# First block's recurrence, index scores and attention in pieces between the parts of its input product, with GpSimd making every second low half from the eighth group on

## The chip, the cores and the metric

The kernel runs on one core of one Trainium2 chip. The metric is the device time of one execution in microseconds; lower is better. The profile is one execution taken by the hardware profiler.

## What is computed

Two transformer blocks, one after the other, on 256 tokens of width 2048, all in float32. The change touches only the first block:

```python
mod = silu(c) @ ada_w + ada_b;  shift, scale, gate = split(mod)
h = rms_norm(x, norm_g) * (1 + scale) + shift
proj = h @ w_in            # 256 x 2048 times 2048 x 9296
a_q, a_k, a_v, a_g, i_q, i_k, i_w, r_q, r_f, r_i, r_g = split(proj)
q, k = rope(rms_norm(a_q)), rope(rms_norm(a_k))       # 8 heads of 128
qi, ki = rope(i_q), rope(rms_norm(i_k))               # 16 index heads of 64
score = sum_h relu(qi_h . ki) * wi_h                  # the 64 best keys of a query are kept
o_a = softmax(q k^T over the kept keys) v * silu(a_g)
o_r = rms_norm(gated recurrence(silu(r_q), lb + (1-lb) sigmoid(r_f), r_i)) * silu(r_g)
x = x + gate * (concat(o_a, o_r) @ w_out)
```

The recurrence is computed in chunks of 64 tokens, with a lower bound lb from a softmax over two rows.

## The kernel before

**Large products.** A product of a 256-row operand with a weight matrix is cut into groups of 512 columns, and a group into 8 parts of 256 rows of the weight (two tiles of 128). SyncE fetches the weight in chunks of 1 MB, two parts each, into a ring `raw` of 4 chunks. To keep float32 accuracy each weight is split: ScalarE writes the rounded high half `w_hi` (`high`, a ring of 4 parts), VectorE writes the rest, the low half `raw_lo` (`low`). TensorE then does 12 matmuls of 128x512 for a part: high times high, low times high, high times low, for two row tiles and two blocks of tokens. ScalarE may be at most four parts ahead of TensorE because of the ring of `w_hi`; VectorE follows ScalarE. Each engine works through its own instruction list in order, and waits on semaphores (`hi_done`, `lo_done`, `mm_done`).

**The input product of the first block** is 19 groups: `g_a` (10), `g_s` (one of only 80 columns) and `g_r` (8), in the order of the columns of `w_in`. In its course VectorE also does, a few instructions after each low half (`Spare` deals them out by a budget in us per part), the gate row of the modulation (64 instructions `gate<-proj,c_sig,gate`, whose chunks of `ada_w` come in through SyncE) and the norms and rotations of queries and keys.

**Behind it, one after the other**, stand the chains of the first block, in which no large product runs: the nonlinear functions over the projected rows on ScalarE, the index scores and the choice of 64 keys (`sc_i`, MAX and MATCH_REPLACE on VectorE), the attention `at1` of 16 steps, then the recurrence: the lower bound (`lb`, with a reciprocal of 128x1024 on VectorE and seven 128x1024 TENSOR_TENSOR on GpSimd), the logarithm `lf`, the cumulative sums on TensorE (`lf,tri`), four times four scalings on VectorE, the turning of `qa`, `ka`, `qb`, and eight heads of small matmuls. Then the output product `g_o` (`w_out`) starts. Its left operand is turned, split and written unit by unit (`turning`, `halves_of`) beside its first group.

Small matmuls write to four banks `pm` in turn; `bank` waits until the reader of four units ago is done.

## Time and profile before

| | |
|---|---|
| median of 3 runs | 2316.65 us (2316.13 to 2317.55) |
| the profiled execution's own time | 2318.26 us |
| its span in the profile | 2316.5 us |
| TensorE busy in the span | 2122.0 us (92%) |
| VectorE busy | 1438.8 us (62%) |
| ScalarE busy | 884.3 us (38%) |
| GpSimd busy | 21.5 us (1%) |

TensorE is nearly always busy, yet its clock is halved in some stretches, and busy time there is longer for the same work. So the table alone doesn't say which stretch can give time back; the windows of the trace do.

### The profile page before, as it was taken

How to read it: one execution, taken by the hardware profiler on the slowest of the kernel's cores; microseconds unless marked ns; L12 is line 12 of the kernel's file. 1: busy time of each engine (PE TensorE's matmuls, PEld its weight loads, DVE VectorE, ACT ScalarE, POOL GpSimd, SP SyncE). 2: the span in 40 equal slices, each digit the busy share in tenths (PEclk: the TensorE clock that was granted, in tenths of full speed). 3: DMA queues.
4: the chain of work that ended last, by engine and by line, in shares of the span. 5: the costliest groups of instructions: out<-in, count | busy, mean ns of one | idle time of the engine just before them, and what ended most of it. 6: DMA issues, size and time to landing. Idle time of an engine off the chain costs nothing.

```text
span 2316.5 us, 23790 instructions
## 1 busy us (share of the span) xinstructions
PE 2122.0 (92%) x9261; PEld 1678.0 (72%) x9261; DVE 1438.8 (62%) x2254; ACT 884.3 (38%) x1070; POOL 21.5 (1%) x13
## 2 busy tenths in 40 slices
PE   6799999996697989999996779898999999999999
PEld 1278888885465867788783458777888888878887
DVE  4478655667837877787778676646544545444443
ACT  1134433444514344344440053435444444443332
POOL 0000000000200000000000000000000000000000
PEclk9889998998767999999997899998999999999999
DMA  9948755553003756576661015454556565655554
GB/s 349 379 164 296 277 190 168 199 192 122 1 1 94 220 156 206 186 223 202 202 198 48 0 37 189 151 188 133 193 186 194 184 196 185 196 167 200 189 193 163
DMA packets 208223, 406.34 MB, mean 175 GB/s; under 512 B 10809, under 2 KB 16369, under 8 KB 207729
## 3 DMA queue, kind: packets, MB, share of 16 engines
q1 hardware_dynamic: 203232, 397.24, 51.9%
q10 hardware_dynamic: 4882, 7.62, 1.0%
q8 instruction: 72, 1.18, 0.2%
q14 instruction: 37, 0.30, 0.0%
HBM read 402.74 MB, written 2.10 MB: 175 GB/s over the span
## 4 chain that ended last, share of the span: by engine, by line
PE 81%; DVE 10%; DMA 5%; ACT 2%; issue 1%; SPq 0%; DVEq 0%; ACTq 0%
PE ps L368 74%; PE pm L438 6%; DMA raw<-in_ada_w 3%; DVE raw_lo L346 2%; DMA raw<-in_w_in 1%; DVE mod_part L986 1%; DVE sc_i L1093 1%; PE pm L722 0%; PE pm L450 0%; ACT w_hi L337 0%; DVE sc_w L1105 0%; DMA decay<-in_decay 0%; DVE f_tmp L1221 0%; DVE xtmp L1336 0%; DVE lb_tmp L1113 0%
## 5 line engine op out<-in xcount | busy, mean ns | idle before, releaser
L346 DVE TENSOR_TENSOR raw_lo<-raw,w_hi 128x1024 fp32r<-128x1024 f32 x648 | 784.8, 1214 | 629.3 <-ACT w_hi L337 621.6
L337 ACT ACTIVATE w_hi<-raw 128x1024 fp32r<-128x1024 f32 x648 | 678.9, 1051 | 973.8 <-PE ps L368 927.6
L368 PE MATMUL ps<-w_hi,h_hi 128*128 128x512 f32 (+1 forms) x2336 | 920.1, 394 | 35.3 <-DVE h_lo L801 19.1
L368 PE MATMUL ps<-raw_lo,h_hi 128*128 128x512 f32 (+1 forms) x2336 | 915.3, 392 | 0.0
L368 PE MATMUL ps<-w_hi,h_lo 128*128 128x512 f32 (+1 forms) x2336 | 914.7, 392 | 0.0
L368 PEld LDWEIGHTS ps<-w_hi,h_hi 128*128 128x128 f32 x2336 | 445.5, 191 | 128.9 <-DVE h_lo L801 21.6
L368 PEld LDWEIGHTS ps<-w_hi,h_lo 128*128 128x128 f32 x2336 | 445.6, 191 | 92.2
L368 PEld LDWEIGHTS ps<-raw_lo,h_hi 128*128 128x128 f32 x2336 | 445.9, 191 | 90.3 <-issue 0.2
L368 PE MATMUL ps<-w_hi,hid_hi 128*128 128x512 f32 x256 | 99.9, 390 | 1.8 <-DVE raw_lo L346 1.8
L368 PE MATMUL ps<-w_hi,hid_lo 128*128 128x512 f32 x256 | 99.6, 389 | 0.0
L368 PE MATMUL ps<-raw_lo,hid_hi 128*128 128x512 f32 x256 | 99.6, 389 | 0.0
L438 PE MATMUL ps<-raw,c_sig 128*1 128x512 f32 x128 | 62.6, 637 | 5.7 <-DMA raw<-in_ada_w 5.7
L986 DVE SCALAR_TENSOR_TENSOR mod_part<-raw,c_sig,mod_part 128x512 f32<-128x512 f32 x56 | 42.1, 752 | 24.9 <-DMA raw<-in_ada_w 23.2
L368 PEld LDWEIGHTS ps<-w_hi,hid_hi 128*128 128x128 f32 x256 | 48.1, 188 | 12.0 <-DVE raw_lo L346 2.1
L368 PEld LDWEIGHTS ps<-w_hi,hid_lo 128*128 128x128 f32 x256 | 48.0, 188 | 9.9
L368 PEld LDWEIGHTS ps<-raw_lo,hid_hi 128*128 128x128 f32 x256 | 48.1, 188 | 9.9
L438 PEld LDWEIGHTS ps<-raw,c_sig 128*1 128x1 f32 x128 | 10.6, 87 | 56.3 <-issue 41.9
L1467 ACT ACTIVATE h_hi<-xtmp 128x256 fp32r<-128x256 f32 x88 | 32.7, 411 | 48.7 <-DVE xtmp L816 21.2
L1011 DVE SCALAR_TENSOR_TENSOR gate<-proj,c_sig,gate 128x512 f32<-128x512 f32 x64 | 47.7, 745 | 0.0
L1223 DVE SCALAR_TENSOR_TENSOR f_tmp<-z_k,w1T,f_tmp 128x128 f32<-128x128 f32 x132 | 46.0, 348 | 2.6
L1495 ACT ACTIVATE proj<-ps 128x1024 f32<-128x1024 f32 (+1 forms) x28 | 28.0, 1000 | 50.4 <-PE ps L368 50.4
L1221 DVE TENSOR_TENSOR f_tmp<-f_tmp 128x128 f32<-128x128 f32 x132 | 35.1, 287 | 1.5
(291 smaller groups left out, 1225.6 us busy)
## 6 DMA issues: line engine op xcount, KB each, us to landing
raw<-in_w_in SPq DMA_DIRECT2D x140, 1024.0 KB, 5.2
raw<-in_w_ffn_gate SPq DMA_DIRECT2D x44, 1024.0 KB, 5.2
raw<-in_w_ffn_up SPq DMA_DIRECT2D x44, 1024.0 KB, 5.1
raw<-in_w_ffn_down SPq DMA_DIRECT2D x44, 1024.0 KB, 5.1
raw<-in_ada_w SPq DMA_DIRECT2D x32, 1024.0 KB, 7.5
raw<-in_w_out SPq DMA_DIRECT2D x32, 1024.0 KB, 5.1
proj<-in_ada_w SPq DMA_DIRECT2D x16, 1024.0 KB, 9.4
raw<-in_w_br_hyena SPq DMA_DIRECT2D x8, 1024.0 KB, 5.0
```

What stands on the lines that cost most here:

```text
L337: nc.scalar.activation(w_hi[:, p % HRING, :, 0:gm.width], raw[:, k % RING, e:e + HT, 0:gm.width], ACT.Copy).then_inc(hi_done, 1)
L346: nc.vector.tensor_tensor(raw_lo[:, k % RING, e:e + HT, 0:gm.width], raw[:, k % RING, e:e + HT, 0:gm.width], w_hi[:, p % HRING, :, 0:gm.wi ...
L368: mm = nc.tensor.matmul(ps[pair][:, t, 0:gm.width], l[:, tok], r[:, i, 0:gm.width], start=(k == 0 and q == 0), stop=(k == kt - 1 and q == 2))
L438: return nc.tensor.matmul(o, l, r, start=start, stop=stop, **kw)
L986: i = v.scalar_tensor_tensor(mod_part[:, b_], raw[:, c, k], w_, mod_part[:, b_], ALU.mult, ALU.add)
L1011: x = v.scalar_tensor_tensor(acc, gate_raw[c][:, k], c_sig[:, CK * c + k:CK * c + k + 1], acc, ALU.mult, ALU.add)
L1093: i = v.scalar_tensor_tensor(sc_i[:, t, 0:nk], sc_r[:, 2 * (n % 2) + r, 0:nk], iw[:, t, head:head + 1], sc_i[:, t, 0:nk], ALU.mult, ALU.add)
L1221: i = v.tensor_tensor(o, x, y, last)
L1223: i = v.scalar_tensor_tensor(o, x, y, last, ALU.mult, ALU.subtract if last is p_ else ALU.add)
L1467: s.activation(h_hi[:, k0 + k], xtmp[:, (k0 + k) % 4], ACT.Copy).then_inc(sig("x_hi"), 1)
L1495: s.activation(dst[:, :, o:o + gm.width], pair[:, :, 0:gm.width], ACT.Copy)\
```

## The change

The first block's input product becomes one `Gemm` of 19 groups in a new order: f, r_q, r_i (two groups each), the narrow one (i_k, i_w), i_q (2), a_q, a_k, a_v, a_g (2 each), r_g (2). Parts are numbered through from 0 to 151; the narrow group is parts 48 to 55, the eighth group begins with part 56. The chains are written as generators that yield the number of the part behind which the next piece stands: TensorE's pieces at the numbers below, VectorE's and ScalarE's `LEAD` = 3 parts later in their own lists (they run ahead of TensorE by about that).

```diff
+GROUPS_IN = ([(R_F + GW * q, GW) for q in range(2)] + [(R_Q + GW * q, GW) for q in range(2)]
+             + [(R_I + GW * q, GW) for q in range(2)] + [(I_K, IDX_D + IDX_H)]
+             + [(I_Q + GW * q, GW) for q in range(2)] + [(A_Q + GW * q, GW) for q in range(8)]
+             + [(R_G + GW * q, GW) for q in range(2)])
+D_AT = (25, 29, 33, 40)
+TURN_AT = (36, 47)
+HEAD_AT = 50
+INDEX_AT = (86, 90, 104)
+QK_AT = 117
+K_SCALED_AT = 118
+AT_AT = 123
+MIX_AT = 145
+LEAD = 3
...
-        g_a = Gemm([(w1v, 0)], KT, 10)
-        g_s = Gemm([(w1v, I_K)], KT, 1, width=IDX_D + IDX_H)
-        g_r = Gemm([(w1v, R_Q)], KT, 8)
+        g_in = Gemm([(w1v, 0)], KT, len(GROUPS_IN), GROUPS_IN)
...
+        shared = (g_in.part(IN_IQ), g_in.end())
+
+        def of_pool(p):
+
+            return shared[0] <= p < shared[1] and p % 2 == 1
...
+        def low_by_pool(pool, gm, j, n):
+            p = gm.part(j, n)
+            if of_pool(p):
+                pool.wait_ge(hi_done, p + 1)
+                low_half(nc.gpsimd, p, gm.width(j)).then_inc(lo_pool, 1)
...
+                if of_pool(p):
+                    pe.wait_ge(lo_pool, pools(p) + 1)
+                else:
+                    pe.wait_ge(lo_done, p + 1 - pools(p))
...
+            beside = Spare(block_one())
+            turn_h1 = turning([("h1", hbuf, KT)])
+            for j in range(g_in.groups):
+                multiply_group(pe, g_in, j, halves, turn_h1 if j == 0 else None, beside if j else None)
...
+            chain, gate_work, head_work = Spare(block_one()), Spare(gate_row()), Spare(queries_and_keys())
+            beside = ((chain, 1e9), (gate_work, 0.7), (head_work, 1.2))
...
-            pool.wait_ge(sig("rg_silu"), 1)
-            pool.wait_ge(sig("gains_in"), 64)
-            for t in range(TT):
-                nc.gpsimd.tensor_tensor(heads(proj, R_G)[:, t], heads(proj, R_G)[:, t],
-                                        gains[:, 3].unsqueeze(1).to_broadcast([P, NH, HD]), ALU.mult).then_inc(sig("rg_gain"), 1)
+            for j in range(IN_IQ, g_in.groups):
+                for n in range(g_in.parts):
+                    low_by_pool(pool, g_in, j, n)
```

The share 1e9 of `chain` means that VectorE and ScalarE do a due piece of the chains whole, however long it is. Further: the sigmoid and silu are applied by ScalarE as it copies a group out of PSUM (`read_in`), so its function changes with the group; the squares of queries and keys go from VectorE to ScalarE, the gains are folded into the rotation tables (`turn_tables`, `rotate_gained`), the key's scale is applied by ScalarE, the query's one in the scores. Six of the eight units of `g_o`'s left operand are turned behind parts 145 to 150. The tables lie elsewhere in memory; `x` is fetched a second time (2 MB) near the end of the product, since its room is used in between. The gate row's chunks have two slots instead of four.

On VectorE the lower bound moves from behind the choice of keys to behind the low half of part 17 (`lb_tmp` before; now the room `xtmp`). Before, around it:

```order
L1106 TENSOR_TENSOR sc_w<-sc_w,sc_i 128x256 [waits v_chain]
L1107 TENSOR_SCALAR sel_add<-sc_w 128x256 [waits v_chain]
L1113 RECIPROCAL lb_tmp<-lb_tmp 128x1024 [waits lb_sum,v_chain]
L1114 TENSOR_TENSOR proj<-proj,lb_tmp 128x1024 [waits v_chain]
L1115 TENSOR_SCALAR proj<-proj 128x1024 [waits v_chain]
```

and now, between the low halves (`raw_lo`) of parts 17 and 18 of the input product:

```order
L380 TENSOR_TENSOR raw_lo<-raw,w_hi 128x1024 [waits hi_done,v_chain]
L1170 RECIPROCAL xtmp<-xtmp 128x512 [waits lb_sum]
L1170 RECIPROCAL xtmp<-xtmp 128x512
L1175 TENSOR_TENSOR proj<-proj,xtmp 128x1024 [waits v_chain]
L1176 TENSOR_SCALAR proj<-proj 128x1024 [waits v_chain]
L1147 SCALAR_TENSOR_TENSOR gate<-proj,c_sig,gate 128x512 [waits v_chain]
L933 TENSOR_TENSOR trig<-sn_rope 128x384 [waits gate_used]
L380 TENSOR_TENSOR raw_lo<-raw,w_hi 128x1024 [waits hi_done,v_chain]
```

The same three steps that stood alone now stand ahead of a low half that TensorE needs, with one gate step and the last rotation table.

On ScalarE, at parts 26 and 27, high halves stand with the copy of group 2 (silu), the logarithm and the exponential, each with its table:

```order
L364 ACTIVATE w_hi<-raw 128x1024 [waits mm_done,landed1]
L1851 ACT_TABLE_LOAD
L1851 ACTIVATE proj<-ps 128x2x512 [waits mm_done]
L1865 ACT_TABLE_LOAD
L1865 ACTIVATE proj<-proj 128x1024 [waits f_ready]
L364 ACTIVATE w_hi<-raw 128x1024 [waits mm_done]
L1865 ACTIVATE proj<-proj 128x1024 [waits f_ready]
L1868 ACT_TABLE_LOAD
L1868 ACTIVATE dec<-pm 128x32 [waits filled]
```

TensorE waits for the second logarithm (`lf_ready`) already behind part 24. Before, the logarithm followed the attention:

```order
L1536 ACTIVATE sc_pT<-pm 128x256 [waits filled] x3
L1657 ACT_TABLE_LOAD
L1657 ACTIVATE lf<-proj 128x1024 [waits f_ready] x2
L1666 ACT_TABLE_LOAD
```

In all, the input product now holds 15 table loads on ScalarE, where it held none. On VectorE at part 73, the output of the recurrence is scaled whole, ahead of the low half of part 74 (that of part 73 is GpSimd's):

```order
L1011 TENSOR_REDUCE hs<-proj 128x2x8 [waits or_sq,gate_step]
L1012 TENSOR_SCALAR hs<-hs 128x2x8 [waits v_chain]
L1014 RECIPROCAL hs<-hs 128x2x8 [waits or_root]
L1235 SCALAR_TENSOR_TENSOR proj<-proj,hs,gains 128x128 [waits gains_in,v_chain]
L1235 SCALAR_TENSOR_TENSOR proj<-proj,hs,gains 128x128 x15
L1147 SCALAR_TENSOR_TENSOR gate<-proj,c_sig,gate 128x512 [waits v_chain]
L380 TENSOR_TENSOR raw_lo<-raw,w_hi 128x1024 [waits hi_done,gate_used]
```

Before, the sixteen stood behind the last head, with no low half waiting. On GpSimd two 128x1024 steps of the r_g gain go, and 48 low halves come:

```order
L2167 TENSOR_TENSOR proj<-proj 128x1024 [waits rf_sig,lb_ready]
L2169 TENSOR_TENSOR proj<-proj 128x1024 [waits f_scaled]
L2167 TENSOR_TENSOR proj<-proj 128x1024
L2169 TENSOR_TENSOR proj<-proj 128x1024 [waits f_scaled]
L380 TENSOR_TENSOR raw_lo<-raw,w_hi 128x1024 [waits hi_done] x48
```

## Rows read from the trace of the kernel before

**Rows 1.** The page: span, busy time, share and instructions of each engine.

```profile
span 2316.5 us, 23790 instructions
...
PE 2122.0 (92%) x9261; PEld 1678.0 (72%) x9261; DVE 1438.8 (62%) x2254; ACT 884.3 (38%) x1070; POOL 21.5 (1%) x13
```

**Rows 2.** Windows: length; busy PE, PEld, DVE, ACT, POOL; clock, DMA share, GB/s.

```profile
128.00:545.30 417.30, 417.23 (x1848) 346.06 (x1848) 282.59 (x377) 171.21 (x181) 0.00 (x0) 0.98 0.63 216
545.30:718.00 172.70, 114.42 (x626) 83.15 (x626) 107.57 (x264) 68.92 (x130) 21.32 (x9) 0.68 0.07 20
718.00:811.30 93.30, 92.71 (x400) 75.68 (x400) 76.71 (x163) 37.75 (x52) 0.00 (x0) 0.97 0.58 184
```

**Rows 3.** The chain that ended last: start, length, what, from the input product on.

```profile
392.87 152.38 PE ps L368 x672
...
595.97 6.57 DVE lb_tmp L1113
...
718.04 5.49 PE ps L368 x12
```

**Rows 4.** Groups by form, 128 to 545 us: busy, mean ns, idle before.

```profile
L346 DVE TENSOR_TENSOR raw_lo<-raw,w_hi 128x1024 fp32r<-128x1024 f32 x140 | 171.5, 1225 | 120.5 <-ACT w_hi L337 119.1
L337 ACT ACTIVATE w_hi<-raw 128x1024 fp32r<-128x1024 f32 x140 | 148.3, 1060 | 195.6 <-PE ps L368 186.6 <-DMA raw<-in_w_in 9.0
...
L1011 DVE SCALAR_TENSOR_TENSOR gate<-proj,c_sig,gate 128x512 f32<-128x512 f32 x64 | 47.7, 745 | 0.0
```

**Rows 5.** Groups of instructions by form, 545 to 718 us.

```profile
L1841 POOL TENSOR_TENSOR proj<-proj 128x1024 f32<-128x1024 f32 x2 | 4.7, 2350 | 13.3 <-DVEq L1116 13.3
...
L1179 DVE SCALAR_TENSOR_TENSOR proj<-proj,hs 128x128 f32<-128x128 f32 x16 | 4.3, 344 | 0.0
...
L1104 DVE MAX8 top<-sc_w 128x8 f32<-128x256 f32 x8 | 3.4, 428 | 0.3
...
L868 DVE TENSOR_REDUCE hs<-qa 128x16 f32<-128x2048 f32 x1 | 2.3, 2286 | 2.0 <-ACT qa L1507 2.0
```

**Rows 6.** Rotation steps of VectorE by form, 128 to 718 us.

```profile
L885 DVE TENSOR_TENSOR xtmp<-proj,trig 128x512 f32<-128x512 f32 x12 | 8.3, 688 | 0.2
...
L888 DVE TENSOR_TENSOR proj<-xtmp 128x256 f32<-128x256 f32 x12 | 5.1, 425 | 0.4
```

**Rows 7.** Timeline, lower bound on VectorE and GpSimd: start, length, what.

```profile
574.98 4.92 POOL L1833 TENSOR_TENSOR proj<-proj,lb_tmp 128x1024 f32<-128x1024 f32 x2 [574.53 <-DVE lb_tmp L1110]
...
602.56 1.23 DVE L1114 TENSOR_TENSOR proj<-proj,lb_tmp 128x1024 f32<-128x1024 f32 x1
603.82 0.69 DVE L1115 TENSOR_SCALAR proj<-proj 128x1024 f32<-128x1024 f32 x1
```

**Rows 8.** VectorE's index score steps of 128x256, 573 to 588 us.

```profile
L1093 DVE SCALAR_TENSOR_TENSOR sc_i<-sc_r,iw,sc_i x16: 480/485/2447, 574.7 to 586.5; 128x256 f32<-128x256 f32 x16
```

**Rows 9.** Chain of waits, the same stretch.

```profile
575.26 2.46 DVE sc_i L1093
...
577.74 2.46 DVE sc_i L1093
...
580.22 0.50 DVE sc_i L1093
```

**Rows 10.** Timeline of ScalarE at the first functions behind the input product.

```profile
548.03 1.91 ACT L1626 ACTIVATE proj<-proj 128x2048 f32<-128x2048 f32 x1
...
549.96 1.28 ACT L1627 ACT_TABLE_LOAD   x1
...
551.26 1.91 ACT L1627 ACTIVATE proj<-proj 128x2048 f32<-128x2048 f32 x1
```

**Rows 11.** Windows of the narrow group (columns as in rows 2).

```profile
350.00:354.00 4.00, 4.00 (x37) 3.93 (x35) 0.97 (x3) 1.93 (x4) 0.00 (x0) 1.00 0.18 41
...
358.00:362.00 4.00, 4.00 (x20) 4.00 (x21) 1.33 (x2) 2.11 (x2) 0.00 (x0) 0.50 0.59 208
...
366.00:370.00 4.00, 4.00 (x12) 3.09 (x12) 1.22 (x1) 1.17 (x2) 0.00 (x0) 0.59 0.75 247
```

**Rows 12.** Window of the first heads of the recurrence.

```profile
656.00:661.00 5.00, 5.00 (x36) 3.22 (x32) 2.09 (x7) 0.00 (x0) 0.00 (x0) 0.50 0.02 3
```

**Rows 13.** TensorE's timeline at the gate row's sums, inside the input product.

```profile
389.27 3.59 PE L438 MATMUL pm<-gate,ones 128*128 128x512 f32 x8
```

More of the change, by code:

```diff
@@ L1064, in queries_and_keys @@
+                dve.sem_inc(sig("ki_roped"), 1)
+                yield g_in.part(IN_IQ + 2, 3)
+                for j in range(2):
+                    evacuated(dve, g_in, IN_IQ + j)
                 for t in range(TT):
@@ new lines, in _ @@
+            mix = halves_in("mix", KT // 2)
+            for n in range(g_in.parts):
+                low(dve, g_in, last, n)
+                for work, share in beside:
+                    work.step(g_in.part(last, n), share)
+                if n >= MIX_AT + LEAD - g_in.part(last):
+                    next(mix)
+            assert chain.over and gate_work.over and head_work.over
+            for n in range(g_o.parts):
+                low(dve, g_o, 0, n)
+                if n == 1:
+                    gate_recurrence(1)
+                if n < 2:
+                    next(mix)
+                if n == 3:
+                    for _ in mix:
+                        pass
@@ new lines, in block_one @@
+            def block_one():
+                yield from recurrence()
+                yield from index()
+                yield from attend_beside()
+            chain, norm_work = Spare(block_one()), Spare(norms())
+            beside = ((chain, 1e9), (norm_work, 1.2))
+            last = g_in.groups - 1
+            for j in range(1, g_in.groups):
+                for n in range(g_in.parts):
+                    high(act, g_in, j, n)
+                    if n == HRING - 2:
+                        read_in(j - 1)
+                    for work, share in beside:
+                        work.step(g_in.part(j, n), share)
+                    if j == last and n >= MIX_AT + LEAD - g_in.part(last):
+                        highs(HT, HT * (n + g_in.part(last) - MIX_AT - LEAD))
@@ L1682, in _ @@
+            assert chain.over and norm_work.over
+            ahead = MIX_AT + LEAD - g_in.part(last)
+            for n in range(g_o.parts):
+                high(act, g_o, 0, n)
+                if n == 0:
+                    read_in(last)
+                if n < 2:
+                    highs(HT, HT * (g_in.parts - ahead + n))
+                if n == 3:
+                    for u in range(g_in.parts - ahead + 2, KT // HT):
+                        highs(HT, HT * u)
             groups(g_o, range(1, g_o.groups), None, squares_of("h2", lambda j: act.wait_ge(sig("h2_added"), j + 1)))
```

875 lines of the change are left out of this document (546 added, 329 removed).

## The prediction, made before the changed kernel had been run

> **What bounds the kernel now.** I read the page first: TensorE is busy for 2122 of 2316.5 us, so little seems to be left [rows 1]. The windows show where it is. In the input product TensorE is busy throughout at a clock of 0.98; then come 172.7 us in which it is busy 114.4 us at a mean clock of 0.68 and the memory is nearly idle (20 GB/s); then the output product runs at full pace [rows 2]. The 172.7 us are the chains of the first block. In the chain that ended last they are a patchwork: a reciprocal of 6.57 us on VectorE, and small matmuls, stand between the last part of one product and the first of the next, which then takes 5.49 us for 12 matmuls where a part in the midst of the product takes 152.38 / 56 = 2.72 us [rows 3]. So the chains wait for each other's latency, and beside the product VectorE and ScalarE have time: of 417.3 us they are busy 282.6 and 171.2 [rows 2].
>
> The profiled execution took 2318.3 us; the sum is made against that. The median of the runs is 1.6 us lower, and I take those off at the end.
>
> **Term 1: the section goes, minus 172.7 us** [rows 2]. Every piece of it now stands between parts of the input product.
>
> **Term 2: its TensorE work stays, plus 81 us.** At full clock the 114.4 busy us at 0.68 are 114.4 x 0.68 = 78 us [rows 2]. Six units of the output product's operand are also turned here; I estimate 3 us for these 24 small transposes. The bounds are 78 and 114 us (the clock as it was). The product's own 152 parts are as many as before, only in another order. Of the output product's 93.3 us, 32 parts need 87; the rest was the half-speed first part and the turning. Afterwards r_g's last group must be copied, multiplied, turned and split beside that first group, and a low half waits behind each of these on VectorE; I take the same 6 us, so nothing changes there.
>
> **Term 3: waits that arise, plus 34 us.** ScalarE can be four parts ahead of TensorE, VectorE about three, which is 8 us of cover. A piece that is longer than the cover stops TensorE.
>
> - *The lower bound, parts 16 to 20: 15 us.* Count from the end of part 13 (time 0). ScalarE makes its high half, loads a table and takes the exponential of 2048 columns: 1.06 + 1.28 + 1.91, done at 4.3 [rows 4, 10]. GpSimd's sum takes 2.35 [rows 5], done at about 7. Behind the low half of part 17 VectorE then does reciprocals (6.57), a product (1.23), a subtraction (0.69) and a gate step (0.745), to 16.3 [rows 3, 4, 7]. Now GpSimd starts four steps of 2.35 us [rows 5], and those stop VectorE: while GpSimd had two such steps, from 574.98 on, two index score steps took 2.46 us each, where the others took 0.50 [rows 7 to 9]. Operations with two inputs in SBUF wait for GpSimd's instruction to end, and one gets in between two. Low halves and gate steps are of that sort. So the low half of part 18 is ready at about 20.5, where TensorE wants it at 4 x 2.72 = 10.9: 9.6 us. The next few alternate with GpSimd and cost some 5 us more. The bounds are 7 (the lock costs nothing) and 20.
> - *Part 24: 4 us.* TensorE waits there for the second logarithm. From the end of part 23 on ScalarE has two table loads (1.28 each), the copy of group 2, a high half and two logarithms (about 1.06 each, as a high half of the same size class): 6.8 us against 2.7 us of cover [rows 4, 10].
> - *Group 9 (parts 72 to 79): 8 us.* VectorE has 4 low halves (4.9), 8 gate steps (6.0), 16 scalings (5.5), the reduction (2.3, and small ones 0.5) and 4 rotations of 2 x 0.69 + 2 x 0.43 (8.9): 28.1 us; with GpSimd's four low halves, which exclude most of these, 9.4 more [rows 4 to 6]. That is 37.5 us against 21.8 us of eight parts. The cover of 8 us is spent once; the rest is 8 us.
> - *Groups 12 and 14: 3 us.* There a choice of keys stands whole (8 MAX and 8 replacements, 7.4 us for 256 keys [rows 5]) ahead of a low half. The same sum gives 28 and 33 us against some 23 and 29 us of TensorE with its pieces, nearly within the cover.
> - *Switches: 4 us*, an estimate for some sixty pieces that are slipped in; between 0 and 8.
>
> In the other groups from the eighth on VectorE and GpSimd together stay below TensorE's time. There the 48 low halves on GpSimd take 59 us off VectorE (48 x 1.225) and cost it no more than the lock. The squares moved to ScalarE and the 15 table loads are hidden: 15 x 1.28 = 19 us on an engine that idled 246 of 417 us.
>
> **Term 4: the clock, plus 16 us.** In the narrow group the granted clock fell from 1.00 to 0.50 while TensorE was busy with matmuls of 80 columns, and rose again only behind it [rows 11]. Now three heads and twelve units of transposes stand in that group as well, and the heads too ran at 0.50 with TensorE busy all the time [rows 12]. Three heads at half clock instead of full cost some 7 us, the rest of the group 4; I take 8 for the chance that it holds. After a stall of some us the first part is slow, as 5.49 against 2.72 shows [rows 3]: three such stalls, 8 us.
>
> Sum: -172.7 + 81 + 34 + 16 = -41.7, so 2276.6 us, and against the median **2275 us**.
>
> **A rule on the table loads.** The load took 1.28 us and stood directly between two activations: the one before ended at 549.94, the load began at 549.96, the next activation at 551.26 [rows 10]. The Trainium skill (ScalarE: Activation LUTs, "What ACT_TABLE_LOAD costs") gives 2.66 us for a switch, with a drain of 1.38 us. By that rule the wait at part 24 would be 2.8 us longer and the time 2278 us. The trace shows no such drain, and the sum goes by the trace.
>
> **Rivals.**
>
> *Less waiting (0.20).* VectorE's list is dealt out finely, and many of its steps read PSUM and would overlap GpSimd. With waits of 20 us and 6 us of clock the time is 2318.3 - 172.7 + 78 + 20 + 6 - 1.6 = 2248 us. For it: 135 us of VectorE's 417 idle before [rows 2]. Against it: pieces such as the reciprocal can't be hidden by 8 us of cover.
>
> *The lock costs more (0.15).* If in the twelve last groups VectorE loses more than the rest of GpSimd's instruction, say a further 0.6 us at each of 48, that is 29 us: 2304 us. For it are the two steps of 2.46 us [rows 9]. The Trainium skill (SBUF — State Buffer, "Who interferes with whom") says that whoever issues first has the shared pair of ports for the whole instruction and the other is blocked, in both directions; the two rows agree for the one direction, and none here shows GpSimd waiting. By that rule a low half on GpSimd can be late too, behind one of VectorE's 1.2 us; it has two parts of cover, so this is this rival's price and not more.
>
> *The weights come late (0.10).* SyncE now waits, ahead of a group's first chunk, for a gate slot that VectorE frees in the same group. Seven groups by 3 us make 2296 us.
>
> *Slower (0.10).* TensorE's clock stays at half in wide parts too, because the slipped-in pieces are of the kind that ran at 0.50 [rows 12]. A wide part then costs 2.72 us more. 42 us are won, so 17 such parts out of some 90 between parts 25 and 144 decide it; thirty give 2357 us. Against it: the four sums of the gate row stood inside the product at 389.27 [rows 13], and the whole window has 0.98 [rows 2]; they were dense, though, and the heads are not.
>
> **How the numbers follow.** The forecast of 2262 to 2296 us has 0.45, the rivals 0.20, 0.15, 0.10 and 0.10. All but the last are faster than before, and I leave 0.03 for a sum of mishaps that ends within 0.2%, which is about what a measurement of this kernel can tell from no change: faster 0.87, same 0.03, slower 0.10. The range reaches from the lower case, with some of its own spread, to the costlier lock: 2243 to 2308 us. That leaves out the slower case and the tails, somewhat under 0.2.
>
> **What the profile would show.** Right: no long stretch with memory idle between the input and the output product; the product's window about 550 us long instead of 417; the longest waits of TensorE at part 18 (for VectorE's low half, 8 to 10 us), at part 24 (for ScalarE's `lf`) and at part 74; VectorE's low halves with a maximum near 2.4 + 1.2 us where the median stays at 1.22; GpSimd busy some 130 us; the clock at 0.5 around the narrow group. Wrong: many low halves at 3 us or more throughout groups 7 to 18 (the lock), waits for `raw` chunks at each group's start (the weights), or a clock under 0.9 over the wide parts behind part 56. What would make the prediction wrong most easily is the size of term 3, which is put together from single pieces of a list that I can read but whose overlap I can't.

## The result, and the profile after

Over 20 runs the changed kernel takes 2296.39 us in the median (2287.4 to 2303.63); the kernel before takes 2315.13 us (20 runs, 2295.54 to 2318.95). The ratio is 0.9945, with a 95% interval of 0.9925 to 0.9965: faster by 0.55%, some 13 us. (The kernel before has two groups of times, of which more below, and its median lies in the upper one; the means of the 20 runs are 12.6 us apart, the medians 18.7.) The forecast was 2275 us. The direction is right and the range holds the time, but more than half of the forecast gain is missing.

The page of the changed kernel, the lines that answer to [rows 1] and two groups of instructions behind them:

```profile
span 2295.3 us, 23865 instructions
...
PE 2114.4 (92%) x9261; PEld 1662.7 (72%) x9261; DVE 1425.7 (62%) x2168; ACT 903.0 (39%) x1157; POOL 139.1 (6%) x59
...
L380 POOL TENSOR_TENSOR raw_lo<-raw,w_hi 128x1024 fp32r<-128x1024 f32 x48 | 120.3, 2508 | 364.0 <-ACT w_hi L364 364.0
...
L1147 DVE SCALAR_TENSOR_TENSOR gate<-proj,c_sig,gate 128x512 f32<-128x512 f32 x64 | 65.5, 1023 | 1.8 <-DVE proj L1176 0.2
```

TensorE's busy share is what it was. The second group is already a sign: the same 64 gate steps took 745 ns each before [rows 4] and take 1023 ns now.

The windows answer to [rows 2], with their columns. The first is the whole input product with its pieces, up to ScalarE's copy of the last group. Then come the windows of four groups, from copy to copy (parts 16 to 23, 24 to 31, 48 to 55 and 72 to 79), and then the groups from the eighth on:

```profile
128.00:697.00 569.00, 527.45 (x2483) 418.99 (x2484) 376.49 (x563) 255.30 (x396) 138.89 (x55) 0.93 0.49 169
...
181.00:224.00 43.00, 27.06 (x106) 21.21 (x105) 35.48 (x27) 10.14 (x10) 10.85 (x4) 0.80 0.43 148
224.00:263.00 39.00, 34.05 (x132) 27.04 (x131) 22.70 (x28) 19.18 (x23) 0.00 (x0) 0.82 0.45 160
...
315.50:343.30 27.80, 27.80 (x209) 24.19 (x208) 14.89 (x30) 8.56 (x16) 2.45 (x1) 0.72 0.56 196
...
414.90:443.90 29.00, 20.96 (x81) 16.42 (x79) 28.52 (x40) 9.15 (x11) 11.70 (x4) 0.82 0.35 119
...
343.30:697.00 353.70, 336.26 (x1603) 264.77 (x1604) 222.24 (x368) 165.17 (x283) 117.89 (x47) 0.96 0.48 162
```

The idle section is gone, but product and pieces take 569.0 us where the product and the section took 417.3 + 172.7 = 590 us [rows 2]. Everything else is equal: what comes before the product takes 128 us in both, and what follows takes 2295.3 - 697 = 1598.3 us now and 2316.5 - 718 = 1598.5 us before, the output product included. So the whole miss lies in these 569 us; the forecast's terms put them at 417.3 + 81 + 34 + 16 = 548.3.

Where TensorE stood shows in its timeline (start, length, what; in brackets the idle time before, and what ended it):

```profile
160.23 0.67 PE L419 MATMUL ps<-w_hi,h_hi 128*128 128x512 f32 x1 [3.08 <-DVE raw_lo L380]
185.49 0.50 PE L419 MATMUL ps<-w_hi,h_hi 128*128 128x512 f32 x1 [1.60 <-DVE raw_lo L380]
202.87 0.80 PE L419 MATMUL ps<-w_hi,h_hi 128*128 128x512 f32 x1 [14.34 <-DVE raw_lo L380]
229.89 6.98 PE L500 MATMUL pm<-ind,proj 128*128 128x2 f32 x32 [4.96 <-ACT proj L1865]
424.73 0.79 PE L419 MATMUL ps<-w_hi,h_hi 128*128 128x512 f32 x1 [7.98 <-DVE raw_lo L380]
518.27 0.80 PE L419 MATMUL ps<-w_hi,h_hi 128*128 128x512 f32 x1 [4.96 <-DVE raw_lo L380]
575.76 0.50 PE L419 MATMUL ps<-w_hi,h_hi 128*128 128x512 f32 x1 [3.43 <-DVE raw_lo L380]
```

These seven are 40.4 of the 41.5 us that TensorE is idle in the window. They are at parts 9, 17, 18, behind part 24 (for the logarithm, L1865), at part 74, and behind the two choices of keys. The first matmul of 512 columns behind a wait takes 0.50 us where the granted clock is still 1.00, as at 575.76; 0.79 to 0.80 shows that the clock was halved meanwhile (0.50 at 202.5, 424.5 and 518.0 us).

### The profile page after: what moved, and what is told of

Same layout as the page of the kernel before. It is cut to its first block, busy times and chain, and to the rows that moved or that the text cites. A ratio compares the mean times of both kernels' runs of the same rounds, so it can differ in the third digit from the quotient of the medians.

```text
span 2295.3 us, 23865 instructions
## 1 busy us (share of the span) xinstructions
PE 2114.4 (92%) x9261; PEld 1662.7 (72%) x9261; DVE 1425.7 (62%) x2168; ACT 903.0 (39%) x1157; POOL 139.1 (6%) x59
## 4 chain that ended last, share of the span: by engine, by line
PE 69%; DVE 10%; DMA 2%; ACT 1%; issue 1%; SPq 0%; DVEq 0%; ACTq 0%
PE ps L419 64%; PE pm L500 3%; DVE raw_lo L380 2%; DMA raw<-in_w_in 1%; DVE sc_i L1254 1%; DVE gate L1147 0%; ACT w_hi L364 0%; PE pm L861 0%; DVE xtmp L1577 0%; DVE f_tmp L1462 0%; DVE xtmp L1578 0%; DVE xtmp L1579 0%; DMA decay<-in_decay 0%; DVE xtmp L1340 0%; DVE proj L1267 0%
## 5 line engine op out<-in xcount | busy, mean ns | idle before, releaser
L380 DVE TENSOR_TENSOR raw_lo<-raw,w_hi 128x1024 fp32r<-128x1024 f32 (+1 forms) x600 | 731.1, 1222 | 609.5 <-ACT w_hi L364 601.3
L364 ACT ACTIVATE w_hi<-raw 128x1024 fp32r<-128x1024 f32 (+1 forms) x648 | 677.7, 1050 | 935.3 <-PE ps L419 872.0
L419 PE MATMUL ps<-w_hi,h_hi 128*128 128x512 f32 (+1 forms) x2336 | 935.7, 401 | 70.8 <-DVE raw_lo L380 55.8
L380 POOL TENSOR_TENSOR raw_lo<-raw,w_hi 128x1024 fp32r<-128x1024 f32 x48 | 120.3, 2508 | 364.0 <-ACT w_hi L364 364.0
L1147 DVE SCALAR_TENSOR_TENSOR gate<-proj,c_sig,gate 128x512 f32<-128x512 f32 x64 | 65.5, 1023 | 1.8 <-DVE proj L1176 0.2
```

Source lines behind the costliest of these rows:

```text
L364: nc.scalar.activation(w_hi[:, p % HRING, :, 0:gm.width(j)], raw[:, k % RING, e:e + HT, 0:gm.width(j)], ACT.Copy).then_inc(hi_done, 1)
L380: return engine.tensor_tensor(raw_lo[:, k % RING, e:e + HT, 0:width], raw[:, k % RING, e:e + HT, 0:width], w_hi[:, p % HRING, :, 0:width]. ...
L419: mm = nc.tensor.matmul(ps[pair][:, t, 0:gm.width(j)], l[:, tok], r[:, i, 0:gm.width(j)], start=(k == 0 and q == 0), stop=(k == kt - 1 and ...
L1147: x = v.scalar_tensor_tensor(acc, gate_raw[i % 2][:, k], c_sig[:, CK * c + k:CK * c + k + 1], acc, ALU.mult, ALU.add)
```

## The experiments

Times are medians. The label in brackets is the name that later texts use. The experiments ran in three batches; the kernel before, run beside each, took 2316.89, 2317.21 and 2314.48 us, so times are compared across batches as they are. Most versions from `lb_dealt` on have four executions only, up to some 10 us apart, and a difference of a few us between two of them is weak evidence. The changed kernel, run again beside the last three as the yardstick:

> The changed kernel, unchanged, as the yardstick for the three beside it: 2292 to 2300 us, as in its first 20 runs.

It took 2297.21 us (10 runs, 2293.84 to 2302.55).

**The kernel before, once more** (`before_again`). No edit.

> The kernel before, unchanged, with a second profile. Its times fall into two groups, near 2298 and near 2316 us, and the profile that the prediction read was of the upper one. If the difference lies in the granted clock of the section behind the input product (0.68 there), this profile, when it falls in the lower group, shows that section some 18 us shorter at a higher clock and everything else as before; the true gain of the change is then half of what the two profiles say. If it falls in the upper group again it shows 172.7 us for the section, and nothing is learnt.

It fell into the lower group: 2301.61 us, span 2299.8. The two windows of 665 to 680 us, of the profile that the prediction read and of this one, and the eight heads in this one's chain of waits:

```profile
665.00:680.00 15.00, 15.00 (x86) 9.68 (x86) 4.87 (x15) 0.00 (x0) 0.00 (x0) 0.50 0.00 1
```

```profile
665.00:680.00 15.00, 15.00 (x154) 10.19 (x152) 8.17 (x25) 0.00 (x0) 0.00 (x0) 1.00 0.01 2
```

```profile
656.82 28.32 PE pm L438 x256
```

The same 256 matmuls of the heads took 46.67 us from 653.67 on in the first profile (its chain of waits), all at a clock of 0.50, and 28.32 us here at 1.00. These 18.35 us cover the 16.65 by which the two executions differ (the rest of the section took some 2 us more in the second). So the kernel before wins some 17 us in about half of its executions by itself (9 of its 20 times are under 2303 us, 11 over 2314), and the gain read from two profiles, 21 us, is larger than the 13 us of the ratio.

**GpSimd makes no low halves** (`no_pool`).

```diff
-        shared = (g_in.part(IN_IQ), g_in.end())
+        shared = (g_in.end(), g_in.end())
```

> GpSimd makes no low halves; VectorE makes all. VectorE gets 48 x 1.22 = 59 us more and is free of GpSimd's interference behind part 55. Theory of lumps (TensorE's waits come from long pieces that stand whole ahead of a low half): the waits at parts 18 and 24 stay as they are, those behind part 56 change by a few us either way: 2290 to 2302 us. Theory of the lock (the interference costs what the offload gains, or more): the waits at parts 74, 103 and 122 shrink and the time falls to 2280 to 2290 us. Rival, that the offload is needed: VectorE's load in group 9 passes TensorE's time by more, and the time rises to 2305 to 2320 us.

2290.03 us (2276.92 to 2295.0), 6 to 7 us less than with GpSimd: the offload costs time. Of the waits that the theory of the lock named, two shrank and the last did not: 7.98 us at part 74 became 3.59, 4.96 behind the first choice of keys became 3.60, and 3.43 behind the second stayed at 3.38. In the groups from the eighth on TensorE is idle for 347.70 - 336.38 = 11.3 us where it was for 17.4, which covers the gain. The rows of TensorE at part 74 and behind the first choice, of this kernel:

```profile
418.99 0.80 PE L419 MATMUL ps<-w_hi,h_hi 128*128 128x512 f32 x1 [3.59 <-DVE raw_lo L380]
508.12 0.80 PE L419 MATMUL ps<-w_hi,h_hi 128*128 128x512 f32 x1 [3.60 <-DVE raw_lo L380]
```

The window of the same groups, and VectorE's costliest forms in them (columns as in [rows 4]), first of this kernel:

```profile
342.30:690.00 347.70, 336.38 (x1603) 265.37 (x1603) 231.68 (x415) 165.25 (x283) 0.00 (x0) 0.97 0.49 164
```

```profile
L380 DVE TENSOR_TENSOR raw_lo<-raw,w_hi 128x1024 fp32r<-128x1024 f32 x95 | 115.8, 1224 | 69.3 <-ACT w_hi L364 67.7
L1147 DVE SCALAR_TENSOR_TENSOR gate<-proj,c_sig,gate 128x512 f32<-128x512 f32 x20 | 14.9, 747 | 0.8
...
L1254 DVE SCALAR_TENSOR_TENSOR sc_i<-proj,iw,sc_i 128x256 f32<-128x256 f32 x16 | 7.7, 483 | 4.1 <-ACTq L1923 3.8
...
L1288 DVE SCALAR_TENSOR_TENSOR proj<-pm,hs,sc_i 128x256 f32<-128x256 f32 x8 | 3.9, 482 | 3.7 <-PE pm L500 3.7
```

and then of the changed kernel:

```profile
L380 DVE TENSOR_TENSOR raw_lo<-raw,w_hi 128x1024 fp32r<-128x1024 f32 x48 | 62.2, 1297 | 60.2 <-ACT w_hi L364 59.3
L1147 DVE SCALAR_TENSOR_TENSOR gate<-proj,c_sig,gate 128x512 f32<-128x512 f32 x21 | 25.3, 1205 | 1.0
...
L1254 DVE SCALAR_TENSOR_TENSOR sc_i<-proj,iw,sc_i 128x256 f32<-128x256 f32 x16 | 14.3, 892 | 5.9 <-ACTq L1923 5.5
...
L1288 DVE SCALAR_TENSOR_TENSOR proj<-pm,hs,sc_i 128x256 f32<-128x256 f32 x8 | 3.9, 482 | 10.8 <-PE pm L500 10.8
```

With GpSimd, 115.8 - 62.2 = 53.6 us of low halves leave VectorE, but VectorE is busy for only 231.68 - 222.24 = 9.4 us less. The other 44 us come back as stretched steps, and not in the low halves, where I had looked for them (their mean rises from 1224 to 1297 ns), but in the steps between them: gate steps from 747 to 1205 ns, rotations of queries and keys (L1340) from 687 to 959, scores from 483 to 892. A step that reads one operand from PSUM (L1288) stays at 482 ns. The sixteen scalings (L1235), with all inputs in SBUF, stay at 343 to 351 ns too, but in lb_gate_or, below, four of them take 3.00 us where four others take 1.14: which steps are caught depends on what falls beside GpSimd's.

**Gate chunks fetched once** (`gate_once`).

```diff
-                    dve.wait_ge(gate_landed[i % 2], 16 * (i // 2 + 1))
+                    dve.wait_ge(gate_landed[i % 2], 16)
...
-                    if 0 <= i < ADA_GATE * RING:
+                    if 0 <= i < 2:
```

> Leaves out 14 of the 16 chunks of ada_w that the gate row reads: the two first ones are fetched, and the gate steps reuse them, so that SyncE never waits for a gate slot (14 MB less are fetched; the gate row's values are not the reference's). Theory of late weights (SyncE stood 14.8 us for two gate slots at 197 to 212 us, and the high half of part 22 waited 7.3 us for its chunk, which made the logarithms late): the wait at part 24 (5 us) and the slow stretch behind it (7 us) go, 2283 to 2288 us. Theory of lumps: the logarithms wait for GpSimd's four steps anyway, 2293 to 2299 us.

2291.67 us (2289.08 to 2294.67), between the two: 5 us less. The wait at part 24 fell from 4.96 to 2.66 us and that at part 74 from 7.98 to 6.72, the slow stretch behind part 24 from 14 to 10.5 us, and ScalarE had no wait for a chunk left. Late weights are real and cost about 5 us in the changed kernel. (The edit also fetches 14 MB less; what that alone is worth was not separated from the waits for slots.)

**The lower bound dealt out** (`lb_dealt`).

```diff
-                yield g_in.part(2, 1)
+                yield g_in.part(1, 7)
                 dve.wait_ge(sig("lb_sum"), 1)
-                for q in range(2):
-                    c = slice(q * GW, q * GW + GW)
+                for q in range(4):
+                    c = slice(q * 256, q * 256 + 256)
...
-                    yield 3.3
+                    yield g_in.part(2, q)
...
-                yield g_in.part(1)
+                yield g_in.part(3)
                 yield from rope_angles()
...
-                yield g_in.part(2)
+                yield g_in.part(1, 5)
                 act.wait_ge(sig("lb_less"), 2)
```

> The lower bound is made one group earlier: ScalarE's exponential behind part 13 instead of 16, VectorE's reciprocal in four pieces of 256 columns behind parts 15 to 18 instead of two whole ones behind part 17; the angles of the rotation start with group 3 instead of group 1 to make room. Theory of lumps: the wait of 14.3 us at part 18 and the half-speed part behind it (2.6 us) go, and most of the wait at part 24 with its slow stretch (5 and 7 us): 2272 to 2284 us. Rival, that the chain itself is too long there: GpSimd's four steps and the logarithms are as late as before, the waits only move to part 24, and the time stays at 2290 to 2297 us.

2285.58 us (2284.79 to 2286.44): 11 us less, near the dear end of what the first theory gave. In place of the waits at parts 9, 17 and 18 (19.0 us) there are three smaller ones, of 4.91, 1.62 and 2.39 us at parts 20, 21 and 24: the first from VectorE's steps beside GpSimd's, the last from something new. ScalarE's wait and SyncE's instructions in this kernel's timeline:

```profile
208.75 2.00 ACT L364 ACTIVATE w_hi<-raw 128x1024 fp32r<-128x1024 f32 x2 [18.28 <-DMA raw<-in_w_in]
...
181.30 20.09 SPq L2109 DMA_DIRECT2D proj<-in_ada_w  x2
201.44 7.79 SPq L351 DMA_DIRECT2D raw<-in_w_in  x4
```

SyncE stands from 181.30 to 201.39 at two gate chunks, whose slots VectorE frees late, and the weight chunks behind them in its list come that much later. This is the rival of the late weights, at one place and not at seven.

**The same, with the gate chunks sent one by one** (`lb_gate`). SyncE sends a gate chunk behind every second weight chunk, and VectorE uses it four parts later.

```diff
-                    yield g_in.part(i // 2 + 2)
+                    yield 15 + 4 * i
...
-                for i in range(2 * j - 2, 2 * j):
+            def gate_chunk(j, c):
+                i = (4 * j + c - 7) // 2
+                if c % 2 == 1:
                     if 0 <= i < ADA_GATE * RING:
```

> The lower bound dealt out as in lb_dealt, and SyncE's gate chunks no longer stand together behind a group's weights: one stands behind every second weight chunk, and VectorE takes it four parts after it was sent (parts 15 to 78). In lb_dealt the high half of part 21 waited 18.3 us for its chunk while SyncE stood 20.1 us for two gate slots, and TensorE then 8.7 us. Theory of late weights: that wait and most of the 3.4 us for the logarithm go, 2269 to 2277 us. Rival, that the chunks were late only because the gate steps were held up by GpSimd, so that SyncE waits at another place: 2282 to 2287 us.

2274.61 us (2272.8 to 2283.16), 11 us less again. (The expectation names 8.7 us of TensorE's wait for lb_dealt's late chunk, and part 21; 8.68 us is the wait at part 74. The late chunk is that of part 24, and its own wait is the 2.39.) That wait is gone, and the one for the logarithm falls from 3.44 to 2.67 us; on the other hand one of 9.63 us stands at part 20, where more gate steps now fall beside GpSimd's four steps. By the two profiles, 11.1 us apart, some 5 us are idle time of TensorE and some 6 are clock, since there are fewer and shorter stalls to restart from. They don't come from one place: the groups of the late chunk and the logarithm are 4.6 us shorter, the two around part 74 are 6.8, and 2.5 us lie ahead of the first edited instruction and are not the edit's. Something unlooked-for comes with it: in place of 7.98 us at part 74 (8.68 in lb_dealt) TensorE waits 1.12 there, 1.87 at part 76 and 1.82 at part 80. There are as many gate steps in the two groups around it (12), but they stand elsewhere. In the changed kernel three of them, stretched to 4.33 us, stood ahead of the sum that ScalarE's root waits for; ScalarE was held for 6.84 us, and its high halves with it. Now the three stand behind the scalings, and ScalarE is held for 2.68 us. The rows of ScalarE, of the changed kernel and of this one:

```profile
413.82 0.22 ACT L1892 ACTIVATE hs<-hs 128x16 f32<-128x16 f32 x1 [6.84 <-DVE hs L1012]
```

```profile
393.31 0.22 ACT L1894 ACTIVATE hs<-hs 128x16 f32<-128x16 f32 x1 [2.68 <-DVE hs L1014]
```

**And the output of the recurrence scaled in pieces** (`lb_gate_or`). ScalarE's root moves from behind part 73 to behind part 75 with it.

```diff
+                at = HEAD_AT + 2 * NH + 1 + LEAD + 3 + 3
+                yield at
+                dve.wait_ge(sig("or_root"), 1)
...
                         if h % 4 == 3:
-                            yield 1.2
+                            at += 1
+                            yield at
```

> lb_gate, and the scaling of the recurrence's output is dealt out: ScalarE's root stands behind part 75 instead of 73, VectorE's reciprocal and sixteen scalings stand behind parts 76 to 83, four at a time, instead of whole at part 73 (the sums lie in a tile of their own). ScalarE stood 6.8 us for VectorE's sum there and TensorE 8.0 us for the low half, and its next part was slow (2.6 us). Theory of lumps: 8 to 11 us less than lb_gate. Rival, that group 9 is overloaded as a whole (37.5 us of VectorE and GpSimd against 21.8): the wait moves on to part 78 or 80, and the gain is 0 to 4 us.

2280.47 us (2275.33 to 2281.94), in the median 6 us more, though the four times of each overlap; the gain of 8 to 11 us did not come. Now TensorE waits 6.11 us at 428.63 us (part 80), in the next group, and that group takes 453.13 - 422.56 = 30.6 us from copy to copy where it took 445.87 - 421.13 = 24.7 in lb_gate. Group 9 itself is 2.3 us shorter, so the edit costs some 3.5 us in the two; the rest of the 6 lies in groups that it doesn't touch. VectorE is busy without a gap from 401 to 431 us there, with rotations, scalings and low halves, several of them stretched by GpSimd. The theory of lumps falls here: a piece that is put off only makes the next ones late, and the wait moves on, as the rival had it. What fills VectorE there, its own work or the stretching, this run can't tell; four_no_pool, below, can.

**And the choices of keys in pieces** (`lb_gate_or_choice`). The four copies of the gate row (`copy_gate`), which stood in a row behind the second choice, are dealt out between its pieces too.

```diff
-                    for _ in range(TOPK // 8):
+                    at = INDEX_AT[1 + t] + IDX_H // 2 + LEAD
+                    for r in range(TOPK // 8):
+                        yield at + r
                         link(v.max(top8[:, t], w))
                         link(v.match_replace(w, top8[:, t], w, REPLACED))
-                        yield 0.7 + 0.3 * t
+                        if t == 1 and r < ADA_GATE:
+                            copy_gate(r)
```

> lb_gate_or, and the two choices of 64 keys are dealt out, one MAX and one replacement behind each part, 101 to 108 and 115 to 122, instead of eight of each whole. TensorE waited 4.7 us near 518 us and 3.4 us at 575.8 us, with slow parts behind. Theory of lumps: 8 to 12 us less than lb_gate_or. Rival (VectorE's total in groups 12 and 14 is the bound, not the lump): 0 to 4 us.

2268.75 us (2267.35 to 2269.79), 12 us less than lb_gate_or, as the theory of lumps gave. Groups 12 and 14 take 24.4 and 28.5 us from copy to copy where they took 32.5 and 34.8, and TensorE's two waits there (4.97 and 3.40 us) are gone. Here the groups had room, and the lumps were in the way; in group 14 the gate copies were part of the lump.

**And GpSimd without low halves** (`four_no_pool`). The edit of no_pool on top.

> lb_gate_or_choice, and GpSimd makes no low halves. With the lumps dealt out, VectorE's total is what is left. Theory of the lock (what GpSimd takes off VectorE, its interference gives back): 0 to 4 us less than with GpSimd. Rival, that dealing out is what makes the offload worth its price, since VectorE now has no spare time in groups 9 to 14: 5 to 15 us more.

2258.46 us (2254.78 to 2263.52), 10 us less, more than either theory gave. Group 10 takes 24.3 us where it took 31.7, and the wait of 6.12 us at part 80 is one of 1.39. So VectorE, with all the low halves on it, has room for groups 9 and 10: what filled it in lb_gate_or was not its own work but that work stretched beside GpSimd's. The rows of TensorE at part 80, of lb_gate_or_choice and of this kernel:

```profile
424.33 0.77 PE L422 MATMUL ps<-w_hi,h_hi 128*128 128x512 f32 x1 [6.12 <-DVE raw_lo L383]
```

```profile
422.81 0.47 PE L422 MATMUL ps<-w_hi,h_hi 128*128 128x512 f32 x1 [1.39 <-DVE raw_lo L383]
```

What is left of TensorE's waits for low halves, in this kernel's list of waits (total, times, longest), is above all one of 9.67 us at part 20. There three gate steps take 8.43 us and a low half 3.25 beside GpSimd's four steps on the forget rows:

```profile
PE ps L419 <- DVE raw_lo L380: 35.7, 7, 14.3
```

```profile
PE ps L422 <- DVE raw_lo L383: 15.8, 7, 9.7
```

The first of the two lines is the changed kernel's, the second this one's.

**GpSimd's four steps on VectorE, alone** (`f_alone`). On the changed kernel; the four steps go from GpSimd's list.

```diff
-                dve.sem_inc(sig("lb_ready"), 1)
+                at = g_in.part(2, 2)
+                yield at
+                dve.wait_ge(sig("rf_sig"), 1)
+                for t in range(TT):
+                    f = kc[:, t]
+                    link(v.tensor_tensor(f, f, lb[:, 1], ALU.mult))
+                    yield at + 2 * t + 1
+                    v.tensor_tensor(f, f, lb[:, 0], ALU.add).then_inc(sig("f_ready"), 1)
+                    yield at + 2 * t + 2
```

> One edit on the changed kernel: GpSimd's four steps on the forget rows (10.9 us in all, at 194.0 to 205.0 us) are done by VectorE, one behind each of parts 18 to 21. Four of VectorE's steps stretched to GpSimd's ends there: 2.87, 2.58, 3.25 and 2.86 us where they take 0.75, 0.56, 1.23 and 0.75. Theory of the lock: 8.3 us of stretching go and 4.9 us of work come, of which most is hidden; the wait of 14.3 us at part 18 falls to 8 to 10 us and the time to 2287 to 2292 us. Rival, that the stretching was only waiting that VectorE had to do anyway (the reciprocals are the lump): 2294 to 2299 us.

2294.82 us (2290.77 to 2298.13) beside 2297.21. The wait at part 18 fell to 8.09 us, as the theory of the lock had it, but the time lies in the rival's range. A wait of 2.95 us for a low half has come in behind it, at part 24. In the two profiles the input product with its pieces is 4.9 us shorter (the last copy at 692.17 us for 697.07), and some 3.5 us more are spent behind it, where the edit changes nothing. So the medians say less than the waits do, and what the stretching costs the whole time stays open here. The timeline of VectorE, GpSimd and SyncE in the changed kernel, and then of VectorE and ScalarE in this one, from behind the reciprocals and their product to the low half of part 18:

```profile
194.04 2.34 POOL L2167 TENSOR_TENSOR proj<-proj 128x1024 f32<-128x1024 f32 x1 [13.57 <-DVEq L1177]
194.05 2.87 DVE L1147 SCALAR_TENSOR_TENSOR gate<-proj,c_sig,gate 128x512 f32<-128x512 f32 x1 [0.15 <-DVE proj L1176]
196.45 2.67 POOL L2169 TENSOR_TENSOR proj<-proj 128x1024 f32<-128x1024 f32 x1
196.95 14.80 SPq L2109 DMA_DIRECT2D proj<-in_ada_w  x2
196.96 2.58 DVE L933 TENSOR_TENSOR trig<-sn_rope 128x384 f32<-128x384 f32 x1
199.08 2.65 POOL L2167 TENSOR_TENSOR proj<-proj 128x1024 f32<-128x1024 f32 x1
199.57 3.25 DVE L380 TENSOR_TENSOR raw_lo<-raw,w_hi 128x1024 fp32r<-128x1024 f32 x1
```

```profile
193.39 0.75 DVE L1147 SCALAR_TENSOR_TENSOR gate<-proj,c_sig,gate 128x512 f32<-128x512 f32 x1
194.18 0.56 DVE L933 TENSOR_TENSOR trig<-sn_rope 128x384 f32<-128x384 f32 x1
194.77 1.22 DVE L380 TENSOR_TENSOR raw_lo<-raw,w_hi 128x1024 fp32r<-128x1024 f32 x1
...
215.01 2.00 ACT L364 ACTIVATE w_hi<-raw 128x1024 fp32r<-128x1024 f32 x2 [10.27 <-DMA raw<-in_w_in]
```

In the first, each of VectorE's steps ends about its own length behind the end of one of GpSimd's (196.92 against 196.38, 199.54 against 199.12, 202.82 against 201.73), and takes 2.87, 2.58 and 3.25 us where the second shows 0.75, 0.56 and 1.22. SyncE's 14.80 us stand in the same stretch. In the second the stretching is gone, but SyncE still stands for gate slots, so the next chunk is late (10.27 us) and takes part of the gain back. The Trainium skill (SBUF — State Buffer, "Who interferes with whom") says that the one that issues first has the shared ports for its whole instruction, and the other is blocked, in both directions; it says this of VectorE's two-port modes, and of a step with two inputs in SBUF that it contends with GpSimd's reads. The rows agree for VectorE. They bear out the other direction too: GpSimd's first step takes 2.34 us, the next two, which start while one of VectorE's ends, 2.67 and 2.65.

**All of it together, but with the scaling whole** (`best`). lb_gate, the choices in pieces, no low half on GpSimd, the forget rows on VectorE behind parts 21 to 24.

> four_no_pool with the forget rows' four steps on VectorE (behind parts 21 to 24), so that GpSimd runs only the three sums of the lower bound, and with the scaling of the recurrence's output whole again as in the changed kernel. Theory of the lock: the wait of 9.7 us at part 20 (VectorE's steps stretched to GpSimd's ends) falls under 2 us, and its slow part goes (3 us): 2245 to 2251 us, less what the whole scaling saves (0 to 6 us by lb_gate against lb_gate_or), so 2240 to 2251. Rival, that the logarithms now come too late, since VectorE makes the steps later than GpSimd did: the wait moves to part 24, 2254 to 2260 us.

2251.07 us (2250.5 to 2253.31), the dear end of the first theory. Two edits were made at once, so the 7 us below four_no_pool are not split between them. TensorE's waits for low halves from 150 us on are down to 6.9 us in 7, the longest 1.4:

```profile
PE ps L421 <- DVE raw_lo L382: 6.9, 7, 1.4
```

**And the heads behind the narrow group** (`best_heads`). The sums of the recurrence's output get a tile of their own (`om`) as well, as in lb_gate_or.

```diff
-HEAD_AT = 50
+HEAD_AT = 58
...
-                m = head_scale("or", qa, NH, HD)
+                m = om[:]
```

> best with the eight heads of the recurrence behind parts 58 to 74 instead of 50 to 66, so that none stands in the narrow group, whose clock was 0.5 for some 20 us. Theory that the slipped-in heads lengthen the slow stretch at the narrow group (my term of 7 us for three heads at half clock): 4 to 8 us less than best. Rival: the narrow group falls to half clock by itself as in the kernel before, and the heads only fill time that is short: within 3 us of best, or a few us more since VectorE's load moves into group 9.

2244.38 us (2241.44 to 2246.88), 6.7 us less. A window around the narrow group, of best and then of best_heads:

```profile
290.00:330.00 40.00, 40.00 (x252) 31.95 (x252) 22.73 (x43) 9.07 (x14) 0.00 (x0) 0.70 0.53 181
```

```profile
290.00:330.00 40.00, 40.00 (x240) 34.61 (x239) 26.52 (x45) 14.72 (x23) 0.00 (x0) 0.83 0.78 267
```

The clock falls in both, but for a shorter time where the heads are not in it: 24.0 us at 0.50 in best, 13.5 in best_heads. The busy time lost to the clock there is 12.0 and 6.8 us, and the product of the kernel before lost the same 6.8. So the narrow group falls to half clock by itself, as the rival said, and the heads lengthen the stretch, as the theory said; some 5 of the 6.7 us are this. This is the fastest version: 0.9708 of the kernel before (0.9656 to 0.9759).

## Why the prediction was right in kind and wrong in size

The mechanism was right: the section goes, its work stays, and some of it comes back as waits and as clock. What failed are sizes. I took the input product in windows of 2 us, multiplied the busy time in each by what its clock lacks to 1.00, and summed. That splits the 569.0 us of the changed kernel: idle 41.5, lost to the clock 29.5, and the remaining 498.0 are work at full clock. For the product before, the same sums are 0.1, 9.7 and 407.5. The forecast in these terms has idle 0.1 + 30, clock 9.7 + 16 = 25.7, and work 407.5 + 81 + 4 for the switches = 492.5. So the miss of 20.5 us (2295.3 + 1.8 = 2297.1 for the profiled execution, against 2276.6) is some 11 us of waits, 4 of clock and 5 to 6 of work. Measured by the gain the miss is larger: 42 us were forecast and some 13 came. Of the 29 us between, 21 are this, and 8 are the kernel before, which was taken at 2316.65 us and has a mean of 2308.8 over 20 runs.

The steps that failed are these. Term 3 held each group's load against TensorE's time and passed the choices of keys as nearly within the cover, where the length of one piece decided (3 us forecast, 8.4 measured), and it had nothing at part 9 (3.1), where GpSimd's two subtractions hold VectorE. It also took GpSimd's low halves to cost VectorE no more than the lock. They took 53.6 us off VectorE and stretched its other steps by 44, and without them the kernel is 6 to 7 us faster. Term 2 was too small by 5 to 6 us, and term 4 lacked the slow stretch behind part 24.

- **Term 1, the section goes.** Right in the sum. But it lasts 172.7 us in half of the executions only; in the second profile it is some 16 us shorter, since the heads run at 1.00. I had read their 0.50 as theirs by kind. That doesn't touch the forecast of a time, but it does the forecast of a gain.
- **Term 2 and the switches: 5 to 6 us too low.** 78 us came from a mean clock that counts idle time too. By windows of 2 us the section's work is 76.6 us in the first profile and 80.0 in the second, and inside the product it is 498.0 - 407.5 = 90.5 with the six turned units. What a piece that is slipped in costs beyond its matmuls was not isolated by a run and stays open. That nothing changes behind the product was right (1598.3 against 1598.5 us).
- **Term 3, the waits: 41 us for 30.** By places:
  - *Parts 16 to 20*: 15 forecast, 1.60 + 14.34 = 15.9 measured. The sum was right, partly by luck, for its parts were not: I had 9.6 us at part 18 and 5 behind it, and it all came at part 18. I let the lock begin behind the gate step, and left the last rotation table out, though the listing showed both; they were stretched (2.87 and 2.58 us) ahead of the low half.
  - *Part 24*: 4 forecast, 4.96 measured, but about half for another reason, a late chunk. With gate_once 2.66 us are left.
  - *Group 9*: 8 forecast, 7.98 measured. The agreement is luck in part. VectorE has hardly a gap there (28.52 of 29.00 us), as I had summed, but more than half of the wait hangs on GpSimd's low halves (3.59 us without them), and where it falls depends on the order too (1.12, 1.87 and 1.82 us at parts 74, 76 and 80 in lb_gate). ScalarE's root, which ties its high halves to VectorE's sum, was not in my account.
  - *Groups 12 and 14*, the choices of keys: 3 forecast, 4.96 + 3.43 = 8.4 measured. **This is the step that failed most clearly.** I compared a group's load with its time and found it "nearly within the cover". But the groups had room, and it was the length of the choice (6.0 us from 507.80 to 513.77, for 128 keys) ahead of a low half that stopped TensorE. In pieces, together with the gate copies, both waits go. GpSimd has a smaller part in the first (3.60 us without its low halves).
  - *Part 9*: nothing forecast, 3.08 measured. Four short steps of the rotation's angles took 5.44 us there, beside GpSimd's two subtractions for the lower bound; away from GpSimd, behind part 24 in lb_dealt, they take 0.27 us each, and the wait is gone. These steps have one full-width input in SBUF (the other is one value per row), and I had let the lock hold only steps with two. The rows of the changed kernel, and then of lb_dealt:

```profile
153.48 5.44 DVE L1317 TENSOR_SCALAR trig<-inv_f,pos_f 128x96 f32<-128x96 f32 x4
153.51 4.72 POOL L2159 TENSOR_TENSOR proj<-proj,xtmp 128x1024 f32<-128x1024 f32 x2 [153.06 <-DVE xtmp L1165]
```

```profile
213.54 1.19 DVE L1317 TENSOR_SCALAR trig<-inv_f,pos_f 128x96 f32<-128x96 f32 x4
```

- **Term 4, the clock: 20 us for 16.** The time at 0.50 around the narrow group grew from some 14 us [rows 11] to 20, which is 3 us of loss for my 8. In best the stretch is 24 us long and loses 5 more than before the change; why it is longer there than in the changed kernel stays open. Missing in my sum was a stretch of 14 us at 0.50 behind part 24, in which the logarithm's small products stand; it costs 6.2 us. The restarts cost 1.6 to 2.7 us each, as forecast, but there were five of them and not three.

Of the rivals, *the weights come late* is real at about 5 us in this kernel (and a part of the 11 us between lb_dealt and lb_gate), where 21 were priced: SyncE stood for gate slots in nearly every group, but ScalarE was far enough ahead at most. *The lock costs more* is real at 6 to 10 us, where 29 were priced; it doesn't lie in the low halves, but in other steps between them. To these come the stretched steps at parts 9 and 17 to 20, beside GpSimd's other work. *Slower* did not come: in the wide groups the clock was 1.00 but for some us behind each stall. *Less waiting* (2248 us) did not come with this order of pieces; best_heads, at 2244 us, shows that the room for it was there.

The rule on table loads had no run of its own. In the profile after, a load of 1.28 us begins at 225.59, behind a copy that ends at 225.57, and the logarithm begins at 226.89, so there is no drain to be seen here either. The same holds for each of the 15 loads of the product: it begins 0.01 or 0.02 us behind the instruction before it. The Trainium skill (ScalarE: Activation LUTs, "What ACT_TABLE_LOAD costs") gives 1.38 us for one; the rows decide.

## What to carry to other kernels

When work is slipped in between the parts of a product, two sums are needed for each engine: its load per group against TensorE's time, and the longest piece ahead of a step that TensorE needs against the cover; either can be the bound. Here dealing out helped against the second (12 us with the choices of keys) and not against the first. Ask what an offload does to the engine that it relieves: here GpSimd took 54 us off VectorE and gave 44 back through steps that nobody had moved. And a wait for a free slot in a DMA queue's list holds back every transfer behind it, so put it where the slot is free already.

## What the runs showed of the hardware

- Some steps of VectorE with all inputs in SBUF were stretched beside GpSimd's to 1.4 to 2.4 times in the mean (rotations 687 to 959 ns, scores of 128 keys 349 to 839). The low halves were stretched little (1224 to 1297 ns), and a step with one input in PSUM was not (482 ns in both kernels). A step of 128x96 with one full-width input, in SBUF, took up to 2.50 us beside GpSimd's and 0.27 away from them.
- The same 256 small matmuls took 46.67 or 28.32 us, depending on the execution, at a granted clock of 0.50 or 1.00, in one and the same kernel.
- At each of the stalls of 3 us and more the granted clock fell to 0.50 and stayed there for 3 to 6 us of dense work, at 576.9 us only after the work had begun again; behind the one at part 24, where small products follow, for 14 us, idle time included.
